# Two weight chunks of the first expert item, each loaded by sixteen transfers of eight partitions

## What is computed

```python
def moe_swiglu(xn, w_router, w_gu, w_down):
    logits = (xn @ w_router).astype(jnp.float32)
    top_v, top_i = lax.top_k(logits, TOP_K)
    top_w = jax.nn.softmax(top_v, axis=-1)
    gates = jnp.sum(jax.nn.one_hot(top_i, N_EXPERTS, dtype=jnp.float32) * top_w[..., None], axis=-2)
    out = jnp.zeros(xn.shape, jnp.float32)
    for e in range(N_EXPERTS):
        out = out + gates[..., e:e + 1] * swiglu(xn, w_gu[e], w_down[e]).astype(jnp.float32)
    return out.astype(xn.dtype)
```

## Time and profile before

| | us |
|---|---|
| median of 3 runs | 1377.17 |
| lowest and highest of them | 1374.26, 1377.53 |
| the profiled execution's own time | 1375.29 |
| its span, first to last instruction | 1373.5 |

### The profile page before, as it was taken

One profiled execution on the slowest core, in us unless ns is written; L12 is line 12 of the kernel. 1 busy time (PEld: TensorE's weight loads), 2 busy tenths in 40 slices (PEclk: granted clock), 3 DMA queues, 4 the chain that ended last, 5 costly groups with the idle time before them and its releaser, 6 DMA issues.

```text
span 1373.5 us, 34667 instructions
## 1 busy us (share of the span) xinstructions
PE 1311.0 (95%) x15450; PEld 829.1 (60%) x15450; DVE 471.1 (34%) x720; ACT 305.6 (22%) x491; POOL 103.7 (8%) x142
## 2 busy tenths in 40 slices
PE   7999999999999898999999999999889999999977
PEld 7999999999895574356443444345334345345423
DVE  6986465555567843111130121112112112103102
ACT  6735443334447841000000000000000000000000
POOL 0500100000402623100000000000000000000000
PEclk9999999999998999999999999999999999999999
DMA  9853365555895046999999999999999999999995
GB/s 294 263 171 107 130 213 183 184 184 182 143 255 196 28 160 243 401 405 383 419 418 417 418 418 418 419 418 418 419 419 418 418 419 417 419 418 411 416 419 230
DMA packets 126907, 436.39 MB, mean 318 GB/s; under 512 B 11235, under 2 KB 72908, under 8 KB 126770
## 3 DMA queue, kind: packets, MB, share of 16 engines
q1 hardware_dynamic: 125218, 430.00, 80.5%
q0 software_dynamic: 1376, 4.13, 2.1%
q10 hardware_dynamic: 176, 0.14, 0.0%
HBM read 431.22 MB, written 1.44 MB: 315 GB/s over the span
## 4 chain that ended last, share of the span: by engine, by line
PE 78%; SPq 9%; DMA 6%; DVE 3%; ACT 2%; issue 1%; POOL 0%; DVEq 0%; ACTq 0%
PE ps L1713 77%; SPq L722 6%; SPq L725 3%; DMA ring<-in_moe_w_gu 2%; DMA silu_g<-in_moe_w_gu 2%; DMA more<-in_moe_w_down 2%; DVE arena L1476 1%; DVE arena L1479 1%; DMA ring<-in_a_w_in 1%; ACT x_hi L908 1%; POOL arena L835 0%; PE ps L2017 0%; ACT arena L1118 0%; ACT x_hi L938 0%; DVE w_lo L535 0%
## 5 line engine op out<-in xcount | busy, mean ns | idle before, releaser
L1713 PE MATMUL ps<-ring,arena 128*32 128x448 f32 (+2 forms) x2722 | 268.7, 517 | 7.3 <-DMA ring<-in_moe_w_gu 5.2
L1713 PE MATMUL ps<-more,arena 128*32 128x256 f32 (+1 forms) x3450 | 264.0, 457 | 4.4 <-DMA more<-in_moe_w_gu 3.2
L1676 DVE TENSOR_TENSOR arena<-arena,ps 128x448 f32<-128x448 f32 x48 | 29.8, 621 | 611.2 <-PE ps L1713 607.8
L1713 PEld LDWEIGHTS ps<-more,arena 128*32 128x32 f32 x3450 | 117.0, 110 | 140.8 <-issue 95.1
L1713 PEld LDWEIGHTS ps<-ring,arena 128*32 128x32 f32 (+1 forms) x2722 | 97.4, 110 | 160.3 <-issue 130.6
L535 DVE TENSOR_TENSOR w_lo<-ring,w_hi 128x2048 fp32r<-128x2048 f32 x66 | 151.3, 2295 | 77.0 <-ACT w_hi L529 76.9
L1713 PE MATMUL ps<-arena 128*32 128x448 f32 (+7 forms) x2036 | 159.5, 429 | 5.5 <-DMA arena<-in_moe_w_gu 1.9
L529 ACT ACTIVATE w_hi<-ring 128x2048 fp32r<-128x2048 f32 x66 | 125.7, 1910 | 93.5 <-PE ps L1713 89.9
L1713 PEld LDWEIGHTS ps<-arena 128*32 128x32 f32 (+3 forms) x2036 | 72.8, 120 | 80.6 <-issue 60.0
L1189 ACT ACTIVATE arena<-ps 128x448 f32<-128x448 f32 x48 | 26.1, 543 | 369.0 <-PE ps L1713 323.4
L1713 PE MATMUL ps<-x_hi,w_hi 128*128 128x256 f32 x672 | 95.2, 292 | 7.3 <-ACT x_hi L908 5.0
(11 more groups left out here) (276 smaller groups left out, 1247.3 us busy)
## 6 DMA issues: line engine op xcount, KB each, us to landing
ring<-in_moe_w_gu SPq DMA_DIRECT2D x112, 896.0 KB, 23.6
more<-in_moe_w_gu SPq DMA_DIRECT2D x80, 896.0 KB, 23.2
more<-in_moe_w_down SPq DMA_DIRECT2D x64, 896.0 KB, 24.0
arena<-in_moe_w_gu SPq DMA_DIRECT2D x40, 896.0 KB, 23.1
arena<-in_moe_w_down SPq DMA_DIRECT2D x32, 896.0 KB, 23.3
ring<-in_moe_w_down SPq DMA_DIRECT2D x32, 896.0 KB, 23.8
ring<-in_ffn_w_gu SPq DMA_DIRECT2D x22, 1024.0 KB, 5.1
silu_g<-in_moe_w_gu SPq DMA_DIRECT2D x24, 896.0 KB, 24.1
```

Of the source, the lines that this page charges most:

```text
L1676: dve.tensor_tensor(SU[:, a, :], SU[:, a, :], ps[:, b, 0:QUARTER], ALU.mult).then_inc(bank_free[b], 1)
L1713: return pe.matmul(o, w, x, start=start, stop=stop, **kw)
```

## The change

In the first item alone, chunks 24 and 30 are no longer loaded by one transfer of 128 partitions. Each is cut into sixteen transfers of eight neighbouring partitions, issued one behind the other by SP; all sixteen count on a semaphore of their own, one for each of the two chunks, and PE waits for all sixteen before it uses the chunk. The other chunks and items load as before; the counts that PE waits for at those two places are one transfer lower, since the place's own semaphore no longer counts this chunk.

```diff
 PER_ITEM = len(ITEM)
+BY_ROWS = (24, 30)
+ROW_PIECE = 8
 LAG = 4
...
         loose_ready = [sem(f"loose_ready{n}") for n in range(len(loose))]
+        row_ready = [sem(f"row_ready{n}") for n in range(len(BY_ROWS))]
...
             v, ready, before = chunk_slot(m)
+            for n, r in enumerate(BY_ROWS):
+                if isinstance(i, int) and i == 0 and m == r:
+                    eng.wait_ge(row_ready[n], 16 * (P // ROW_PIECE))
+                    return v
+                if r % DEEP == m % DEEP and (m > r or not (isinstance(i, int) and i == 0)):
+                    before -= 1
             eng.wait_ge(ready, 16 * (before + m // DEEP + 1) + i * (16 * PER_ITEM // DEEP))
...
                     slot_free(m, i)
+                    if isinstance(i, int) and m in BY_ROWS:
+                        at = (ED if kind == "up" else 0) + WIDE * j
+                        src = w_dn[:, j, WIDE * q:WIDE * q + WIDE] if kind == "dn" else w_gu[:, q, at:at + WIDE]
+                        for r in range(0, P, ROW_PIECE):
+                            sp.dma_start(v[r:r + ROW_PIECE, :], src[r:r + ROW_PIECE, :]).then_inc(row_ready[BY_ROWS.index(m)], 16)
+                        continue
                     if kind == "dn":
```

## The result

| | before, us | after, us |
|---|---|---|
| median, 8 runs each, taken together | 1376.47 | 1387.21 |
| lowest and highest | 1373.8, 1377.67 | 1380.81, 1391.16 |
| the profiled execution | 1375.29 | 1385.3 |
| its span | 1373.5 | 1383.5 |

The changed kernel is slower: the ratio is 1.0073, with a 95% interval of 1.0056 to 1.009, or 10.7 us by the medians. In the changed kernel's profile line 734 issues the pieces, lines 737 and 740 are the old 722 and 725, and PE's line 1713 is 1728.

The account below looks back on a forecast made before the run. From 553 to 650 us transfers were taken to wait for PE to free places; from 655 us nothing is unused. PE 0, SP 0 and engines 0 to +3.6 us gave a forecast of 1377.5 us, range 1373 to 1392.

Parts of the forecast that it names:

- PE's waits and its 27 us in hand: First item: chunks 24 and 30 land 27 us before PE uses them, so later issue and changed waits cost PE 0.
- SP's issues: At the two chunks: sixteen issues of 0.41 us take 6.6 us, next chunk 4.3 us late, caught up within three chunks; 0.
- The engines, the price of a piece: Eight engines carry the pieces at SP's pace, 4.4 us more a chunk; 8.8 less 5.2 unused, 3.6 us late at 650.
- 5.2 unused: In 553 to 650 us transfers run at 394 GB/s against 418 later, leaving 5.2 us of transfer time unused.
- The other eight engines, "I count nothing": Engines without pieces have sixteen rows fewer, 4.4 us, but a backlog of at most 2.6 us; gain counted as nothing.
- What is made up: Behind 650 us: if other engines carry the instruction fetches, lateness up to 10 us is gone by the end.
- Narrow pieces: Rival at 555 to 605 us: neighbouring partitions make pieces slow, 1.07 us each, 24.6 us late; 1392 or 1402; chance 0.40.
- Relief: Rival: engines that end last are the ones spared, and their 4.4 us stay saved; 1372.8 us, chance 0.10.
- "right": Sign: sixteen issues of about 0.4 us twice, no PE wait for transfers before 650 us, last landing near 1362.7 us.
- "wrong (narrow)": Sign: chunk 24 landing 20 us behind issue, PE waiting early in the second item, last landing 8 us or more later.

Follow-up runs that it names:

- the issues with their waits alone: Against the kernel before: chunks 24 and 30 each by one transfer of 1784 columns and sixteen small ones of eight columns; 1376.1 us, ratio 0.9999.
- The two early chunks: The change's pieces of eight on chunks 3 and 6 instead of 24 and 30; 1375.67 us, ratio 1.0006 to the kernel before.
- the even and odd ones: Against the kernel before: chunks 24 and 30 each in two transfers of 64 partitions, one the even, one the odd partitions; 1375.9 us, ratio 1.0002.
- the spread pieces: The change with the eight partitions of each piece lying four apart instead of neighbouring; 1380.31 us, ratio 1.0028 to the kernel before.
- one chunk's 4.5 us: The change with only chunk 24 in pieces of eight, chunk 30 by one transfer; 1375.68 us, ratio 0.9993 to the kernel before.
- the run meant for it: Against the kernel before: six chunks, each by one transfer of 112 partitions and sixteen of one row; 1398.52 us, ratio 1.0173.
- the kernel with four chunks: The change's pieces of eight on chunks 24, 30, 36 and 42 instead of two chunks; 1392.95 us, ratio 1.013 to the kernel before.

## Why the prediction was wrong in its likeliest case

**PE's waits and its 27 us in hand.** Right: PE is busy 90.00 us of 90 in the first item, and the issues with their waits alone measure 0.9999.

**SP's issues.** Right: 0.34 us where 0.41 was taken, caught up in three chunks. What the sum leaves out is what the other engines do meanwhile (below).

**The engines, the price of a piece.** This is the step that failed: "I take this value: the big loads of this queue are nearer than the narrow ones in queue, row length and order". The value was SP's pace, 0.41 us a piece, 4.4 us a chunk more. The dips give 0.63 to 0.70 us, 10 to 11.3 a chunk in place of 2.19, some 8.5 more. The two early chunks give the same 0.63 us with SP's pace excluded, since SP issues a piece each 0.34 us there. That pieces of eight are slow because their partitions are neighbours is shown in part: for 64 partitions by the even and odd ones, for eight by the spread pieces, which take two thirds of the engine time. The narrow loads of the earlier trace rows were the nearer row for that. Two chunks cost 17 us more; less the 5.2 unused, about 12 late, against 3.6 in the sum. That is for the engines that carry the pieces; from chunk 24 on the end lost 10.3.

**The other eight engines, "I count nothing".** Wrong as well, though the size is bounded only. If eight engines alone were 12 us late, the bytes missing at 653 us would be half of that, 6 us; 9.2 are missing. In the first dip a part of this is SP's: it issues no whole chunk for 5.4 us, and the busy share falls to 0.64 from 555 to 560 us. The text saw that a backlog of 2.6 us is all that these engines have, but not that they run dry behind it. In the second dip the share is 1.03 for 180 GB/s, so the other engines are not idle there but slowed. The views name no engine; what slows them is open.

**What is made up.** The 5.2 us unused before 650 us were worked out rightly: one chunk's 4.5 us disappear within 0.6 us. That up to 10 us could be made up behind 650 us if other engines fetch instructions was not borne out: 9.2 us are missing at 653 us, and the end loses 10.3; against the estimated 12 us for the engines that carry the pieces, that leaves about 2 us that can have been made up. Which engines fetch stays open, since the run meant for it starved PE.

**The rivals.** Narrow pieces came, at the place and, as far as shown, by the cause that the text gives, at a lower price than 1.07 us. Its 24.6 us of lateness were too many, and its 1392 came near 1387.2 only because the two errors, price and making up, have opposite signs. Relief did not show: the last landing is later, not earlier. The median lies in the range; the forecast of 1377.5 and its own range of 1375 to 1381 missed it.

**The signs named ahead.** The issues and PE's steady work came as "right", the 70.45 us of work in 80 early in the second item and the last landing 10.2 us later as "wrong (narrow)". Chunk 24 was not 20 us behind its issue: its dip ends by 566.25 us, 13 us behind it.

## What to carry to other kernels

Cut a load by columns, or by every other partition, rather than into blocks of neighbouring partitions: here two chunks so cut lost 0.7 us (four column pieces) and 0.5 us (even and odd partitions) by one profile each, blocks of 16 to 64 cost 3 us, blocks of eight 10. Judge a transfer by the bytes in narrow slices, not by the busy share of the engines, which stood at 1.03 while they moved 180 GB/s instead of 398. Unused transfer time hides a first such delay whole and the next hardly at all, so a test with one instance can show nothing where two cost 10 us.

## What the runs showed that was not expected

- Blocks of 16, 32 and 64 neighbours lose about alike (2.8, 3.6 and 3.2 us from chunk 24 on), blocks of eight three times as much in the change (10.3), but not in the kernel with four chunks, where the dip of a chunk lacks about half as much as in the change (3.2 to 3.8 us against 6.4 to 7.3).
- The rule cited in the prediction from "SBUF — State Buffer" in the Trainium skill made an estimated 1.05 us of a piece of eight; 0.63 to 0.70 were measured. The measurement decides; what the pieces gain over the rule, the views don't show.
- An issue on SP of eight partitions four apart takes 0.67 us, of eight neighbours 0.34.
